# The gate tiles of the merge computed inside the recurrent stage

## The reference, cut to what matters

```
n = modulate(rmsnorm(x, norm_g[l, 1]), shift[:, 1], scale[:, 1])
qa, kva, ga, qb, fb, ib, gb, ma, mb = jnp.split(n @ w_in[l], splits, axis=-1)
o_a, new_win = nsa_mixer(qa, kva, sigmoid(ga), ...)          # attention, 512 wide
o_b, s_new = hgrn2_mixer(qb, fb, ib, gb, lb[l], s0, gain)    # recurrence, 512 wide
merged = jax.nn.sigmoid(ma) * (o_a @ w_branch_nsa[l]) + jax.nn.sigmoid(mb) * (o_b @ w_branch_hgrn[l])
x = x + gate[:, 1] * (merged @ w_out[l])
```

## Time and profile before

| | |
|---|---|
| median of 3 runs | 3728.57 us (3725.07 to 3730.02) |
| the profiled execution, its own time | 3729.18 us |
| its span, first to last instruction | 3727.4 us |
| mean granted clock of TensorE | 0.915 |
| recurrent stage of layer 0 | 1135.1 to 1277.5 us |
| merge stage of layer 0 | 1277.5 to 1482.3 us |

### The profile page before, as it was taken

One profiled execution on the slowest core, in us unless ns is written; L12 is line 12 of the kernel. 1 busy time (PEld: TensorE's weight loads), 2 busy tenths in 40 slices (PEclk: granted clock), 3 DMA queues, 4 the chain that ended last, 5 costly groups with the idle time before them and its releaser, 6 DMA issues. The chain is left out here.

```text
span 3727.4 us, 60811 instructions
## 1 busy us (share of the span) xinstructions
PE 3307.9 (89%) x23395; PEld 3073.9 (82%) x23395; DVE 1525.1 (41%) x2961; ACT 1150.2 (31%) x1708; POOL 55.3 (1%) x32
## 2 busy tenths in 40 slices
PE   4889998799966898999978999987996779989997
PEld 2689998778745898999966999975884679989997
DVE  2743334325417334333366333342552453343334
ACT  1742223323313233322255322222432313342222
POOL 0000000000002000000000000000000200000000
PEclk6999999889967799999989999987997679999998
DMA  4932323421122132232276232343113202323231
GB/s 75 360 107 85 90 85 116 132 79 49 32 91 77 54 85 79 79 91 85 83 250 208 85 90 85 85 143 111 53 45 97 76 26 79 86 72 90 86 90 64
DMA packets 515217, 359.32 MB, mean 96 GB/s; under 512 B 42858, under 2 KB 469248, under 8 KB 513739
## 3 DMA queue, kind: packets, MB, share of 16 engines
q1 hardware_dynamic: 505580, 343.87, 31.0%
q10 hardware_dynamic: 9472, 13.24, 1.2%
HBM read 335.18 MB, written 30.15 MB: 98 GB/s over the span
## 5 line engine op out<-in xcount | busy, mean ns | idle before, releaser
L188 DVE TENSOR_TENSOR w_lo<-w_raw,w_hi 128x1024 fp32r<-128x1024 f32 (+1 forms) x390 | 469.4, 1204 | 1214.9 <-ACT w_hi L183 1214.7
L183 ACT ACTIVATE w_hi<-w_raw 128x1024 fp32r<-128x1024 f32 (+1 forms) x390 | 406.0, 1042 | 1270.1 <-PE pa L200 597.8
L200 PE MATMUL pa<-nhi,w_hi 128*128 128x272 f32 x1408 | 294.3, 290 | 34.4 <-DVE nlo L243 27.4
L200 PE MATMUL pa<-nhi,w_lo 128*128 128x272 f32 x1408 | 293.5, 290 | 0.0
L200 PE MATMUL pa<-ghi,w_hi 128*128 128x272 f32 x1408 | 291.5, 288 | 1.3 <-DVE glo L824 1.3
L200 PE MATMUL pa<-nlo,w_hi 128*128 128x272 f32 x1408 | 292.4, 289 | 0.0
L200 PE MATMUL pg<-nhi,w_lo 128*128 128x272 f32 x1408 | 292.4, 289 | 0.0
L200 PE MATMUL pg<-nhi,w_hi 128*128 128x272 f32 x1408 | 292.3, 289 | 0.0
L200 PE MATMUL pa<-ghi,w_lo 128*128 128x272 f32 x1408 | 291.4, 288 | 0.0
L200 PE MATMUL pg<-nlo,w_hi 128*128 128x272 f32 x1408 | 291.3, 288 | 0.0
L200 PE MATMUL pa<-glo,w_hi 128*128 128x272 f32 x1408 | 290.2, 288 | 0.0
(11 more groups left out here) (378 smaller groups left out, 5756.1 us busy)
## 6 DMA issues: line engine op xcount, KB each, us to landing
ada_raw<-in_ada_w SPq DMA_DIRECT2D x72, 1024.0 KB, 7.0
w_raw<-in_ffn_w_in SPq DMA_DIRECT2D x352, 192.0 KB, 2.6
w_raw<-in_w_in SPq DMA_DIRECT2D x156, 192.0 KB, 2.7
w_raw<-in_ffn_w_out SPq DMA_DIRECT2D x128, 192.0 KB, 2.5
w_raw<-in_ffn_w_in SPq DMA_DIRECT2D x176, 128.0 KB, 2.6
w_raw<-in_ffn_w_out SPq DMA_DIRECT2D x160, 128.0 KB, 2.3
w_raw<-in_w_in SPq DMA_DIRECT2D x94, 128.0 KB, 2.9
cn<-in_cache_nsa_kv SPq DMA_DIRECT2D x64, 128.0 KB, 2.2
```

The costliest lines, as they stand in the source:

```text
L183: act.activation(self.hi[slot][:, 0:k, :], self.raw[slot][:, 0:k, :], ACT.Copy).then_inc(self.hi_done, 1)
L188: dve.tensor_tensor(self.lo[slot][:, 0:k, :], self.raw[slot][:, 0:k, :], self.hi[slot][:, 0:k, :].bitcast(F32), ALU.subtract).then_inc(sel ...
L200: mm = pe.matmul(out[:, half, 0:HALF], w[slot][:, k0 + n, :], x[:, n, half * HALF:(half + 1) * HALF], start=(n == 0 and w is self.hi and x ...
```

## The change

The 16 gate tiles of a layer move from merge_stage to hgrn_stage.

- SP asks for nhi and nlo first in hgrn_stage, ahead of masks and states. For each gate tile i it loads tile i + 2, waits for the park of tile i and stores that gate (before its sigmoid) to DRAM, m_dram; the 16 loads end with the first two tiles of the merge. The stores of hg_p and hg_s come after all of these.
- TensorE computes the tiles in 32 halves of 24 matmuls: two at each of the 8 positions of ORDER, one after each of the first four turns of k, one in each of the four state steps, one after each of the 8 sample state updates. A tile's first half waits for the split of its weights and for the park of the tile before, since there is one PSUM tile pd of two banks. Inputs are turned one token tile at a time, at positions 1 to 4, through bank 5 alone; the stage's own banks go from 8 to 6.
- ScalarE parks each finished tile (a copy from pd to one of three SBUF places: pj chunk 9, ssq, rs) and then splits the weights of tile i + 2; VectorE's part of the split is placed after its selections and among its later steps.
- merge_stage loads the gates back (2 of 16 first, then 14, ahead of the weights from tile 2 on), applies the sigmoid in SBUF, two gates at a time, and runs 8 branch tiles and 8 of w_out. ohi and olo are made in 8 chunks; the first branch tile follows them chunk by chunk. The PSUM tiles of a branch tile are double. Loops of the merge are written out.

```diff
@@ hgrn_stage, sync
+                    for n, part in enumerate((nhi, nlo)):
+                        sp.dma_start(part..., n_dram[n]).then_inc(n_in, 16)
                     sp.dma_start(level[:, :, :], a["c_level"]).then_inc(mask_in, 16)
...
-                    for n, part in enumerate((nhi, nlo)):
-                        sp.dma_start(part..., n_dram[n]).then_inc(n_in, 16)
+                    for i in range(NG):
+                        if i + 2 < len(tiles_):
+                            wt.load(sp, wt.at(i + 2), tiles_[i + 2])
+                        sp.wait_ge(me_done, i + 1)
+                        sp.dma_start(m_dram[i], parked[i % 3]).then_inc(m_out[i % 3], 16)
                     sp.wait_ge(su_done, 16)
@@ scalar
+                    def park(i):
+                        wt.multiplied(act, wt.at(i))
+                        if i >= 3:
+                            act.wait_ge(m_out[i % 3], 16 * (i // 3))
+                        act.activation(parked[i % 3].rearrange("p (h t) -> p h t", h=2), pd[:, :, 0:HALF], ACT.Copy).then_inc(me_done, 1)
+                        if i + 2 < len(tiles_):
+                            wt.split_hi(act, wt.at(i + 2), DC)
...
                         act.activation(d, bc[:, :, :] if n == NL else d, ACT.Exp).then_inc(e_done, 1)
-                        for t in range(5) if n == 1 else ():
-                            r = TOKT[t][1]
-                            act.wait_ge(tr_done, t + 1)
-                            act.activation(rows[0:r, t, :], bank[5 + t % 2][0:r, 0, :], ACT.Copy).then_inc(ie_done, 1)
+                        if n >= 1:
+                            park(n - 1)
+                        if n < 5:
+                            r = TOKT[n][1]
+                            act.wait_ge(tr_done, n + 1)
+                            act.activation(rows[0:r, n, :], bank[5][0:r, 0, :], ACT.Copy).then_inc(ie_done, 1)
+                    park(8)
+                    park(9)
                     for t in range(5):
+                        if t in (2, 4):
+                            park(9 + t // 2)
...
                     act.activation(g1[:, :, :], ob[:, :, :], ACT.Square).then_inc(sq_done, 1)
+                    for i in range(12, NG):
+                        park(i)
@@ vector
                     for pos, n in enumerate(ORDER[1:]):
                         operands(n)
                         select(ORDER[pos])
+                        if n >= 1:
+                            wt.split_lo(dve, wt.at(n + 1), DC)
                     select(NL - 1)
+                    wt.split_lo(dve, wt.at(8), DC)
...
+                    wt.split_lo(dve, wt.at(9), DC)       # after the last operands
+                        if t in (2, 4):                  # after the copies of k
+                            wt.split_lo(dve, wt.at(9 + t // 2), DC)
+                        if t in (1, 3):                  # after the state updates
+                            wt.split_lo(dve, wt.at(12 + t // 2), DC)
+                        if b % 2 == 1 and 14 + b // 2 < len(tiles_):
+                            wt.split_lo(dve, wt.at(14 + b // 2), DC)
@@ tensor
+                    def half_gate(z):
+                        i, second = divmod(z, 2)
+                        u, slot = wt.at(i)
+                        if z == 0:
+                            pe.wait_ge(n_in, 32)
+                        if not second:
+                            pe.wait_ge(wt.lo_done, 2 * u + slot + 3)
+                            if i >= 1:
+                                pe.wait_ge(me_done, i)
+                        mm = wt.some(pe, slot, pd, nhi, nlo, DC, 4 * second, 4 * second + 4)
+                        if second:
+                            mm.then_inc(wt.mm_done, 1)
...
-                        if n == 0:
-                            turn_inputs(2, 5)
+                        half_gate(2 * pos)
+                        if 1 <= pos < 5:
+                            turn_input(pos)
+                        half_gate(2 * pos + 1)
...
+                        if t < 4:
+                            half_gate(16 + t)            # after each turn of k
+                            half_gate(20 + t)            # in each state step
+                        half_gate(24 + b)                # after each sample state
@@ merge_stage, sync
+                    sp.dma_start(mg[:, 0:2, :], m_dram[0:2].rearrange("n p t -> p n t")).then_inc(mg_in0, 16)
+                    sp.dma_start(mg[:, 2:2 * DC, :], m_dram[2:2 * DC].rearrange("n p t -> p n t")).then_inc(mg_in1, 16)
+                    for t in range(2, 2 * DC + 2):
+                        wt.load(sp, wt.at(t), tiles[t])
@@ scalar
+                    for n in range(DC):
+                        act.activation(ohi[:, n, :], branches[n], ACT.Copy).then_inc(oh_done, 1)
                     for c in range(DC):
+                        act.wait_ge(mg_in1 if c else mg_in0, 16)
+                        act.activation(mg[:, 2 * c:2 * c + 2, :], mg[:, 2 * c:2 * c + 2, :], ACT.Sigmoid).then_inc(sg_done, 1)
+                        wt.split_hi(act, wt.at(c + 2), DC)
+                        act.wait_ge(m_done, c + 1)
+                        act.activation(mhi[:, c, :], m32[:, :], ACT.Copy).then_inc(mh_done, 1)
@@ vector
+                        dve.wait_ge(sg_done, c + 1)
+                        wt.multiplied(dve, wt.at(c))
+                        for z in range(2):
+                            dve.tensor_tensor(two(tt[:, z, :]), two(mg[:, 2 * c + z, :]), pp[c % 2][z][:, :, 0:HALF],
+                                              ALU.mult).then_inc(ta_done, 1)
+                        dve.wait_ge(ta_done, 2 * c + 2)
+                        dve.tensor_tensor(m32[:, :], tt[:, 0, :], tt[:, 1, :], ALU.add).then_inc(m_done, 1)
+                        wt.split_lo(dve, wt.at(c + 2), DC)
+                        dve.wait_ge(mh_done, c + 1)
+                        dve.tensor_tensor(mlo[:, c, :], m32[:, :], mhi[:, c, :].bitcast(F32), ALU.subtract).then_inc(ml_done, 1)
@@ tensor
+                    for c in range(DC):
+                        u, slot = wt.at(c)
+                        pe.wait_ge(wt.lo_done, 2 * u + slot + 3)
+                        if c >= 2:
+                            pe.wait_ge(ta_done, 2 * c - 2)
+                        for n in range(DC):
+                            if c == 0:
+                                pe.wait_ge(ol_done, n + 1)
+                            z, k0 = divmod(n, R)
+                            mm = wt.some(pe, slot, pp[c % 2][z], ohi[:, R * z:, :], olo[:, R * z:, :], R, k0, k0 + 1, R * z)
+                        mm.then_inc(wt.mm_done, 1)
                     pe.wait_ge(ml_done, DC - 2)
+                    pe.wait_ge(ta_done, 2 * DC)
```

More of the change, by code:

```diff
@@ L1568, in _, with gate_tiles, hgrn_stage @@
                         act.activation(pT[:, 0, 0:4, :], pk[0][:, 0, :].rearrange("p (t q) -> p t q", t=4), ACT.Copy).then_inc(ta_done, 1)
-        def hgrn_stage(l, pj, ob, nhi, nlo):
+        def gate_tiles(l):
+            return [wt.columns(DC, a["w_in"][l][:, m + c * P:m + (c + 1) * P]) for c in range(DC) for m in (C_MA, C_MB)]
+        def hgrn_stage(l, pj, ob, nhi, nlo, follow):
             NL = len(LEVELS) - 1
@@ L1602, in hgrn_stage @@
                 inv = sb("inv", [P, 5, HG], at=st)
-                bank = [ps(f"b{i}", 1, st) for i in range(8)]
-                SPREAD = (0, 1, 5, 6, 7)
+                bank = [ps(f"b{i}", 1, st) for i in range(6)]
+                pd = ps("pd", 2, st)
+                SPREAD = (0, 1, 4, 5, 3)
+                gates = gate_tiles(l)
+                NG = len(gates)
+                tiles_ = gates + follow
+                parked = [pj[:, 9, :], ssq[:, :], rs[:, :]]
                 block = st.enter_context(nc.Block())
@@ L1794, in _, with turn_input @@
                 def _(pe):
[L1795 to L1802, removed]
-                    turn_inputs(0, 2)
+                    def turn_input(t):
+                        t0, r = TOKT[t]
+                        if t >= 1:
+                            pe.wait_ge(ie_done, t)
+                        for h in range(HG):
+                            mm = pe.transpose(bank[5][0:r, 0, h * P:(h + 1) * P], ob[:, h, t0:t0 + r], ident[:, :])
+                        mm.then_inc(tr_done, 1)
+                    def half_gate(z):
[10 more added lines that the diff above has]
+                            mm.then_inc(wt.mm_done, 1)
+                    turn_input(0)
                     for pos, n in enumerate(ORDER):
@@ L1910, in _ @@
                 @block.sync
                 def _(sp):
-                    for t in range(2, UO):
-                        c, kind = divmod(t, 3)
-                        wt.load(sp, wt.at(t), merge_tile(l, kind, c))
-                    for c in range(DC):
-                        wt.load(sp, wt.at(UO + c), wt.columns(DC, a["w_out"][l][:, c * P:(c + 1) * P]))
-                    for q, tile in enumerate(follow):
```

(23 more changed lines are left out.)

112 lines of the change are left out of this document (44 added, 68 removed).

## The result

The changed kernel takes 3679.04 us in the median of four runs (3675.47 to 3688.71), beside 3726.82 us (3723.66 to 3730.02) for the kernel before on the same chip: ratio 0.9876, 95% interval 0.9854 to 0.9898. Forecast were 3677 us, from 3653 to 3708. The profiled execution was the longest of the four (3688.71 us), so what follows goes by the lengths of its stages and not by its whole.

What follows compares the result with a forecast made beforehand. TensorE, busy 89% of the span, was taken to bound the merge but not the recurrent stage. Per layer +63.6 and -89.9 give -26.3 us, -52.6 in all from 3729.2: 3677 us, range 3653 to 3708.

Steps and rivals of the forecast that it cites:

- Where the gain comes from: Dense TensorE work leaves the merge, which TensorE bounds, for the recurrent stage, which it doesn't: -89.9 and +63.6 us a layer.
- Prices between other work: Recurrent stage: half tile 3.2 us, 32 products 3.75, small matmuls 0.12 each; levels 0 to 3 42.5, 4 to 6 30.7.
- Wait before the turns of k: Recurrent stage, before the transposes of k: TensorE idles 2.7 us; a low clock after it, +2, only in the upper bound.
- Sample tokens and states: Late recurrent stage: sample tokens 12 + 0.6 us; eight sample states with a half tile each 35.4 us.
- The tail: End of the recurrent stage: 17 us taken against 21.0 before, bounds 15.5 and 21.
- Merge: Merge stage, per layer: -96.0 for 16 gate tiles, +1.3 start, +4 gates' return, +0.8 first output tile: -89.9 us.
- the stall behind the gates' return: Merge start: tile 2's weights land behind the gates; stall 3 us plus 1 for the clock, +4, bounds 0 and 7.
- The rate of the gates' return: Merge start: 4.46 MB of gates at 375 to 409 GB/s take 10.9 to 11.9 us.
- The rival of the ports: Levels: splits on VectorE wait up to 2 us for GpSimd, 7 x 2 = 14 us a layer: 3705 us; chance 0.14.
- The rival of the hand-over: Recurrent stage: the single pd held 1.6 us by each of 16 parks takes the gain of 26.3: 3729 us; chance 0.04.
- The rival of the low clock: Recurrent stage: 32 halves at 1.2 GHz cost 5.8 instead of 3.2 us, +83 a layer: 3843 us; chance 0.06.

Runs made afterwards that it cites:

- b4_nooverlap: Changed kernel with the same 32 half tiles back to back behind the last sample state, none between steps of the recurrent stage: 3771.44 us, 1.0115 of the kernel before.
- b1_queue3: Changed kernel with merge loads queued as gate tiles 0-1, branch tile 2's weights, gates 2-3, tile 3's weights, gates 4-15, later weights: 3666.35 us.
- c2_thin: Changed kernel with three quarters of the products of the first eight gate tiles left out, all parking, splitting, loads and stores kept: 3644.72 us.
- a2_warm: Changed kernel with two of the eight half tiles of the sample states computed between the heads of the sample tokens instead: 3682.85 us.
- b3_bestfill: Changed kernel with finer merge load order, half tiles 23 to 25 between sample-token heads, half 16 in the wait before the turns of k: 3660.36 us.
- a0_again: The changed kernel itself, unaltered, timed again beside the first group of variations: 3679.11 us, 0.9868 of the kernel before.
- a1_queue: Changed kernel with the weights of branch tiles 2 and 3 queued ahead of the 14 gates at the merge's start: 3672.68 us.

## Why the prediction was right, step by step

- **Where the gain comes from: shown.** Dense work moved from a stage that TensorE bounds into one that has waits to fill. b4_nooverlap takes only the place away, and the gain turns into a loss. Of what the place hides, three quarters are idle time; the rest is busy time, for which the clock is the likely reason and is not shown.
- **Prices between other work: all a little too high.** Levels 0 to 3 took 40.0 instead of 42.5 us, levels 4 to 6 30.0 instead of 30.7, the state steps 22.0 instead of 23.8. From start to start a half tile is 3.08 us in the levels and in the state steps, and 3.20, as in attention, between the sample states. The greater part of the error lies in the short matmuls beside it. The forecast took their price from printed lengths (32 in 3.81, 0.12 each), which run past the start of the next group: from start to start 32 products take 3.49, and the 24 small matmuls of a state step 2.6 instead of 3.0.
- **Wait before the turns of k: 2.64 against 2.7**; the turns with their last copy 17.4 against 16.45. The half tile behind this wait took 4.63 us instead of 3.08, at a clock of 0.67 (1236.1 to 1241.2): the low clock after the idle time that the forecast had only in its upper bound (+2) came, at 1.5 us. The start was longer too: the diagonal and its two half tiles took 12.2 us, 11.65 forecast.
- **Sample tokens and states: too low by 2.0 and 1.2.** 14.6 and 36.6 us against 12.6 and 35.4: three of the four heads came at or near the lower clock (3.26, 3.58 and 3.58 us against 1.95), where the forecast took about two, and the first half tiles behind them too. The tail was 17.7 against 17.
- These errors cancel: the stage took 206.2 and 207.2 us, 206.1 forecast. This nearness is luck in part, and so is that of the whole, where the kernel before was 2.4 us below the execution that the sum started from. By layer the two stages saved 21.7 and 23.0 us where 26.3 were forecast, and what is missing is mostly the next term.
- **Merge: -85.4 and -87.8 against -89.9.** Its first matmul comes 1.6 us after the start (1.6), the wait before the first output tile is 1.5 (1.7). The term that was mis-sized is the stall behind the gates' return: +4 was taken for it and the clock after it. TensorE waited 4.5 us, from 15.7 to 20.2 after the start. The weights landed 17.8 us after the start where 15 to 16 was worked out: that sum had the gates and tile 2's weights alone, while tile 3's 0.5 MB moved beside them, about 1.4 us at the rate below (an estimate). With the 6 us at clock 0.50, which cost about 3, the term is 7.5 in layer 0, beyond the forecast's 7 by little. In layer 1 the wait was 3.0. b1_queue3 shows the sum without it: -93.2 and -93.3, where the forecast's sum without its stall is -93.9.
- **The rate of the gates' return.** From 1.6 us after the merge's start the core's DMA engines moved 378 GB/s for 6 us and 384 for 12:

```profile
1345.90:1357.90 12.00, 11.98 (x81) 12.00 (x82) 6.39 (x10) 5.34 (x8) 0.00 (x0) 0.82 1.02 384
```

By that, the 4.46 MB alone take 11.6 to 11.8 us, inside the forecast's 10.9 to 11.9; with the weights between them the transfer of 14 gates landed 16.2 us after its issue. The Trainium skill, DMA: Bandwidth & Descriptors, "Where 436 GB/s comes from", would have about 358 GB/s as the most from HBM to SBUF, half of what two cores share; these stretches of one core alone lie above it, though less than the 409 of the earlier trace rows.
- **The rival of the ports: the effect exists, the cost doesn't arise.** Four of the seven splits in the levels take 2.7 to 3.0 us instead of 1.2, 6 us a layer in all, each within the 2 us that the rival allowed. But this is no new load of 6 us: five of VectorE's first operand products (L1720) took 2.35 to 3.02 us before, and now only two (L1752) are long, 2.77 and 2.31, so about 5 us went from them to the splits. It doesn't reach TensorE, which is busy 69.50 of 69.50 us. c2_thin shows how near it is: with TensorE's work thinned, VectorE bounds at 7.5 us a level. The Trainium skill, SBUF — State Buffer, "SBUF: two separate sides", has VectorE and GpSimd hold their shared ports in turn; that the long splits begin under GpSimd's operations and end 1.1 us after them, about their own length alone, agrees.
- **The rival of the hand-over: refuted here**, with one wait of 0.4 us, since other work of 0.5 us or more stands between two tiles. Where none does, b4_nooverlap pays the 0.8 us at every tile.
- **The rival of the low clock: refuted.** The half tiles ran at 1.00 in the levels and state steps, and the clock was 0.98 from 1158.3 to 1279.1 us, where about 0.95 was forecast. The exceptions are the one behind the wait before the turns of k and the first after the 4-column matmuls.

## What to carry to other kernels

Dense work that one stage is bound by is worth moving into another whose bounding engine is a different one, and the gain is what the place hides, not the work that leaves. Count all of it (here 88 us leave, 109 arrive, 44 are hidden: half of these in waits that were there, a quarter in hand-overs between tiles, and a quarter in busy time, by a higher clock as it seems). What the moved work hands over through DRAM has to be queued by first use, in pieces as small as what waits for them: the one transfer of 14 tiles ahead of a weight tile cost 9.8 us in the two merges and 12.8 in the median (b1_queue3), where the forecast had 8. Price short operations by the distance between starts, not by printed lengths. And where a stage gains 2 us and the next one loses them, look at a second profile of the same kernel before building on it: here it differed by as much.

## What was not expected of the hardware

- The granted clock fell to 0.50 behind 4-column matmuls while TensorE counted as busy for 13.93 of 14.50 us; the earlier trace rows had that already. In the change, a group of 16 takes 1.95, then 3.26, then 3.58 us. New is what half tiles between the groups do: the first three groups in a2_warm and all four in b3_bestfill stay at 1.95, and the half tiles behind them run partly at the lower clock, so that most of the loss stays.
- A stall of 4.5 us at the merge's start was followed by 6 us at 0.50, 26 matmuls where 50 fit. The wait costs its length and about 3 us more behind it; in b1_queue3, without the wait, that stretch has 50 matmuls at 1.00. The price behind a stall is not fixed: in a0_again, after 4.2 us, only the first 3 us are at 0.51 and the next 3 at 0.93, and in a1_queue, after 2.7 us at tile 3, the clock is 1.00.
